# The first three weight slabs of a stage: rounded half of x first, products with the remainder a chunk behind

## The reference

```python
x = layer_norm(DN_ALPHA * x + 0.5 * swiglu(x, ffn1_w_gate[i], ffn1_w_up[i], ffn1_w_down[i]), ...)
y = swa_mixer(x, ...) if kind == 0 else nsa_mixer(x, ...)      # layer 0: sliding window, layer 1: NSA
x = layer_norm(DN_ALPHA * x + y, ...)
x = layer_norm(DN_ALPHA * x + mem_cross_attention(x, mem, ...), ...)
x = layer_norm(DN_ALPHA * x + 0.5 * swiglu(x, ffn2_w_gate[i], ffn2_w_up[i], ffn2_w_down[i]), ...)
```

## Time and profile before

| | |
|---|---|
| median of 3 runs | 2507.37 us (2506.06 to 2510.13) |
| profiled execution | 2509.4 us, span 2507.6 us |
| mean granted clock of PE | 0.964 of full speed |
| PE busy | 2312.6 us, 92% of the span |
| POOL, ACT, DVE busy | 1171.1, 871.6, 839.0 us |
| matmuls | 11164 |

### The profile page before, as it was taken

How to read it: one execution, slowest core, us unless ns; L and a number is a source line. 1 busy time by engine, 2 the same in 40 slices (tenths; PEclk the granted TensorE clock), 3 DMA queues, 4 the chain that set the end, 5 groups by cost and what they waited for, 6 DMA issues and landing times.

```text
span 2507.6 us, 28615 instructions
## 1 busy us (share of the span) xinstructions
PE 2312.6 (92%) x11164; PEld 1942.9 (77%) x11164; DVE 839.0 (33%) x1610; ACT 871.6 (35%) x1505; POOL 1171.1 (47%) x703
## 2 busy tenths in 40 slices
PE   7999997789799799999799999789999798999997
PEld 5888886677687688888688888678887686888886
DVE  2111134456436311113311112446676436211115
ACT  3322233553243322223322223256664243322222
POOL 5454444556446454444354444244446445644442
PEclk9999999999899899999899999899999898999998
DMA  4332332112312233333233332220002312333331
GB/s 162 101 93 93 101 93 85 59 35 76 110 51 84 82 94 101 93 100 93 68 97 97 93 101 89 62 68 18 18 18 69 99 51 76 95 98 97 97 96 56
DMA packets 57734, 204.96 MB, mean 82 GB/s; under 512 B 6912, under 2 KB 7040, under 8 KB 57088
## 3 DMA queue, kind: packets, MB, share of 16 engines
q1 hardware_dynamic: 55728, 196.63, 26.1%
q10 hardware_dynamic: 1872, 6.50, 0.7%
HBM read 201.01 MB, written 2.10 MB: 81 GB/s over the span
## 4 chain that ended last, share of the span: by engine, by line
PE 81%; DVE 8%; POOL 6%; issue 3%; ACT 3%; ACTq 0%; DMA 0%; DVEq 0%; POOLq 0%
PE bank L1211 23%; PE bank L1213 23%; PE bank L1212 23%; POOL w_lo L377 4%; PE bank L1407 2%; DVE t L918 1%; DVE f L894 1%; PE bank L1433 1%; DVE f L886 1%; ACT w_hi L522 1%; PE bank L1434 1%; PE bank L1435 1%; PE bank L1237 1%; PE bank L1239 1%; PE bank L1238 1%
## 5 line engine op out<-in xcount | busy, mean ns | idle before, releaser
L377 POOL TENSOR_TENSOR w_lo<-w_raw,w_hi 128x1024 fp32r<-128x1024 f32 (+1 forms) x379 | 905.0, 2392 | 1055.2 <-ACT w_hi L522 1055.0
L1211 PE MATMUL bank<-x_hi,w_hi 128*128 128x512 f32 x1712 | 681.0, 398 | 78.0 <-DVE memk L937 31.8
L1212 PE MATMUL bank<-x_lo,w_hi 128*128 128x512 f32 x1712 | 676.1, 395 | 0.0
L1213 PE MATMUL bank<-x_hi,w_lo 128*128 128x512 f32 x1712 | 675.7, 395 | 0.0
L522 ACT ACTIVATE w_hi<-w_raw 128x1024 fp32r<-128x1024 f32 (+1 forms) x379 | 390.8, 1036 | 520.5 <-PE bank L1213 504.3
L1211 PEld LDWEIGHTS bank<-x_hi,w_hi 128*128 128x128 f32 x1712 | 327.7, 191 | 149.6 <-POOL w_lo L377 33.6
L1211 PE MATMUL bank<-h_hi,w_hi 128*128 128x512 f32 x960 | 378.7, 395 | 3.7 <-DVE h_lo L1153 2.8
L1213 PEld LDWEIGHTS bank<-x_hi,w_lo 128*128 128x128 f32 x1712 | 327.0, 191 | 69.5
L1212 PEld LDWEIGHTS bank<-x_lo,w_hi 128*128 128x128 f32 x1712 | 327.8, 191 | 64.4
L1212 PE MATMUL bank<-h_lo,w_hi 128*128 128x512 f32 x960 | 374.2, 390 | 0.0
L1213 PE MATMUL bank<-h_hi,w_lo 128*128 128x512 f32 x960 | 374.1, 390 | 0.0
(11 more groups left out here) (197 smaller groups left out, 2620.9 us busy)
## 6 DMA issues: line engine op xcount, KB each, us to landing
w_raw<-w_dram SPq DMA_DIRECT2D x315, 512.0 KB, 3.6
w_raw<-w_dram SPq DMA_DIRECT2D x64, 448.0 KB, 3.3
f<-mem_dram ACTq DMA_DIRECT2D x3, 1024.0 KB, 4.9
t<-x_dram ACTq DMA_DIRECT2D x4, 512.0 KB, 8.4
out_dram<-t SPq DMA_DIRECT2D x8, 256.0 KB, 2.0
f<-cmp_w_dram ACTq DMA_DIRECT2D x1, 1024.0 KB, 6.6
cw<-cmp_w_dram ACTq DMA_DIRECT2D x1, 96.0 KB, 8.7
lng<-ln_g_dram ACTq DMA_DIRECT2D x1, 32.0 KB, 9.3
```

The costliest lines, as they stand in the source:

```text
L377: pool.tensor_tensor(w_lo[:, slot(s), 0:n * P], w_raw[:, s % RAW, 0:n * P], w_hi[:, slot(s), 0:n * P].bitcast(F32), ALU.subtract).then_inc ...
L1211: pe.matmul(dst, w_hi[:, slot(s), w], m_hi[:, k, :], start=k == 0, stop=False)
L1212: pe.matmul(dst, w_hi[:, slot(s), w], m_lo[:, k, :], start=False, stop=False)
L1213: last = pe.matmul(dst, w_lo[:, slot(s), w], m_hi[:, k, :], start=False, stop=k == n - 1)
```

## The change

`together` no longer calls `chunk`. For each chunk k it waits on `xhi_ready` and issues for the three slabs the two products with `x_hi` of chunk k; then it waits on `x_ready` of chunk k - 1 and issues for the three slabs the one product with `x_lo` of chunk k - 1. The loop has a ninth pass, with only the three remainder products of the last chunk; these close the accumulation and raise `slab_done`. The wait on `lo_ready` of a slab stays ahead of its first product. There are 72 products as before, on the same operands; the order in which they are added up in PSUM differs. `together` is called once in each stage.

```diff
--- before.py
+++ after.py
@@ -1220,10 +1220,23 @@
 
             def together(st, group):
 
-                for k in range(KC):
-                    pe.wait_ge(x_ready, KC * st.ln + k + 1)
-                    for s, dst in group:
-                        chunk(s, dst, x_hi, x_lo, k, KC)
+                n0 = KC * st.ln
+                for k in range(KC + 1):
+                    if k < KC:
+                        pe.wait_ge(xhi_ready, n0 + k + 1)
+                        for s, dst in group:
+                            w = slice(k * P, (k + 1) * P)
+                            if k == 0:
+                                pe.wait_ge(lo_ready, s + 1)
+                            pe.matmul(dst, w_hi[:, slot(s), w], x_hi[:, k, :], start=k == 0, stop=False)
+                            pe.matmul(dst, w_lo[:, slot(s), w], x_hi[:, k, :], start=False, stop=False)
+                    if k:
+                        pe.wait_ge(x_ready, n0 + k)
+                        for s, dst in group:
+                            w = slice((k - 1) * P, k * P)
+                            last = pe.matmul(dst, w_hi[:, slot(s), w], x_lo[:, k - 1, :], start=False, stop=k == KC)
+                            if k == KC:
+                                last.then_inc(slab_done, 1)
 
             def token_major(ss, b, i, src_hi, src_lo, width):
```

## The result

The changed kernel takes 2522.22 us (median of 5 runs, 2519.73 to 2524.98), the one before beside it 2508.56 us. The ratio is 1.0055 (95% interval 1.004 to 1.007): slower by 13.7 us, between 10 and 17.6. The profiled execution of after has a span of 2520.2 us, 12.6 more than before, and a mean granted clock of 0.960 in place of 0.964. The forecast was 2514.6 with a range up to 2520: the direction was right, the size is outside the range.

What follows compares the result with a forecast made beforehand. PE, 92% busy, was taken to bound the kernel, starting on x only in stage 7. Terms -1.16 + 3.2 + 2.7 = +4.7 us plus 2.5 for the clock gave 2514.6 us from 2507.4; range 2508.5 to 2520.

Steps and rivals of the forecast that it cites:

- Pace, 0.227 us: In the stage blocks, one product takes 0.227 us at the full clock, across chunk borders and semaphore waits too.
- free semaphore waits: The eight semaphore waits each stage gains cost nothing, because TensorE's queue of issued work hides them.
- (1): Stage 7's start: PE begins on the rounded half of x instead of its remainder, 1.16 us sooner.
- (2): Stop before slab three in seven stages: four products precede it, not six, so 0.45 us each, +3.2 us.
- (3): Slab one released later at the block's end: 0.91 us more in each of stages 1, 2 and 6, +2.7 us.
- slack of 1.8 us in the feed-forward stages: Stages 0, 3, 4, 7: slab four's work covers the late release with 1.8 us to spare, so no cost.
- cover by kw in stage 5: Stage 5: slab kw's product just covers the late release of slab one; 0.1 us at most.
- The rival in which the late slab is swallowed: Stages 1, 2 and 6 have slack behind the late start: only +2.0 us, 2509.4 us; chance 0.15.
- (4): Clock falls behind longer idles: a fall in stage 1 (1.7), half for stages 2 and 6 (0.85), +2.5 us.
- The upper bound, 6.8: Clock cost at most 6.8 us: four falls, both ends of stage 1 and one each in stages 2 and 6.
- the clock falls everywhere: Rival: +4.7 + 6.8 us, with later short idles of the mixers falling too, 2519 us; chance 0.1.
- moved work: The first three terms, at stage 7's start, slab three's stops and slab one's release: +4.7 us without the clock.

Runs made afterwards that it cites:

- e6: Kernel before with, in stages 0 to 6, slabs one and two by chunk and slab three whole behind them; stage 7 in the new order: 2465.93 us, ratio 0.9837.
- e3: Kernel before with only the six middle chunks lagged, first and last chunk whole as before the change: 2508.15 us, ratio 1.0002.
- e2: Changed kernel's start and lag, but the last chunk done whole, slab by slab, so slab one is released as before: 2511.77 us, ratio 1.0017.
- e4: Kernel before with the new order in stage 7 alone: 2504.44 us, ratio 0.9987.
- e5: Changed kernel plus two unread products ahead of slab three's wait, so six stand there again: 2518.7 us, ratio 1.0046.
- g3: Changed kernel plus unread products: two ahead of slab three's wait, 8 behind stage 1's block, 6 behind those of stages 2 and 6: 2514.68 us, ratio 1.0023.
- g1: Kernel before plus four unread products behind the 72 of stage 0, a pure shift of 0.91 us: 2510.67 us, ratio 1.0009.
- g2: Kernel before plus eight unread products behind the 72 of stage 0, a pure shift of 1.8 us: 2505.85 us, ratio 0.9995.
- f2: Kernel before with chunk 0 whole and the rest lagged (late release of slab one) in stages 1, 2 and 6 alone: 2520.24 us, ratio 1.0051.
- f3: As f2, plus unread products behind the block, 8 in stage 1 and 6 in stages 2 and 6: 2516.19 us, ratio 1.0031.
- f1: Kernel before with the late release of slab one in all stages but 1, 2 and 6: 2507.95 us, ratio 1.0002.
- e1: Kernel before with chunk 0 whole and the rest lagged in all stages, so slab one is released late: 2519.25 us, ratio 1.0037.

## Why the prediction was right or wrong

**What bounds the kernel: right.** The change names x, and x was not what PE waits for at seven of eight starts. The waits for weight remainders decided, as `e6` shows from the other side.

**Pace, 0.227 us, and the free semaphore waits: right.** `e3` has the lagged middle and is the kernel before within 0.1%. In after, 51 products behind the stop of stage 4 take 0.227 us each. The 1 us that the range's upper end holds for the semaphore waits is a term that no run shows; `e3` has 48 of the 64 additional waits and bounds them at 2.8 us.

**(1) Stage 7: right.** The first product came 1.94 us behind the start of the rounding of its `x_hi` before (2125.59 against 2123.65) and comes 0.77 us behind it after (2138.32), 1.17 sooner where 1.16 was predicted:

```profile
2137.55 0.72 ACT L619 ACTIVATE x_hi<-t,lnb 128x512 fp32r<-128x512 f32 x1 [3.91 <-DVE t L918]
```

It is 0.77 or 0.78 us in the traces of `e2`, `e4`, `e5` and `g3` as well.

**(2) 0.45 us at each of seven stops: right where it can be seen alone, hidden by the clock elsewhere.** In stage 2 of `g3` and `e5` it is there to the hundredth together with (3). In stages 3, 4 and 5 of after it isn't: the shift is the same behind them as ahead of them. The stop of stage 4 is 0.85 us longer (7.86 against 7.01), because four products end sooner than six, and it ends at the same moment. But the clock came back sooner behind it. (In stage 6 the end of the stop wasn't set by ScalarE and GpSimd alone, as the prediction had it, but in before by the raw slab's DMA too.) In stage 3, first the product at the stop and the 30th behind it in before, then the same two in after:

```profile
831.24 0.79 PE L1211 MATMUL bank<-x_hi,w_hi 128*128 128x512 f32 x1 [3.17 <-POOL w_lo L377]
...
840.98 0.39 PE L1211 MATMUL bank<-x_hi,w_hi 128*128 128x512 f32 x1
```

```profile
842.99 0.80 PE L1231 MATMUL bank<-x_hi,w_hi 128*128 128x512 f32 x1 [4.02 <-POOL w_lo L377]
...
852.25 0.39 PE L1232 MATMUL bank<-x_hi,w_lo 128*128 128x512 f32 x1
```

The same 30 products take 9.74 us before and 9.26 after, 0.48 less, which is what the two additional ones cost. The prediction's clause that they come at the full clock "since the low phase behind a stop passes first" held the low phase to be the same in both orders. Kernels with before's order in stage 3 have it too: these 30 products take 9.47 to 9.49 us in `e4`, `g1` and `g2`, 9.26 in `f2` and 9.23 in `f3`. So the gain needs no change of the order; a term of 0.45 us is smaller than what the clock does behind such a stop from one execution to the next.

**(3) The late release: right as work.** 0.91 us in each of stages 1, 2 and 6 shows in the idles (3.17, 2.39, 2.40, against 2.27, 1.49 and 1.49), and `f1` shows no cost elsewhere, so the slack of 1.8 us in the feed-forward stages and the cover by kw in stage 5 held. The rival in which the late slab is swallowed falls.

**(4) The clock: the step that failed.** It stood in the sum at 2.5 us, the rest in the table is 7.9 of the profiled execution, and 9.0 of the median's 13.7. The prediction's sentence was "I take the first as a fall (1.7) and half a fall for the two together (0.85)". That much was nearly right: 3.17 us of idle in stage 1 gave a fall in each of the four profiled executions that have it, of 1.5 us in after, `e1` and `f2` and of 2.5 in `e5`; 2.27 gave none in seven, and 1.39 none in two. 2.39 to 2.40 gave one of 1.5 in stage 6 in four of four, none in stage 2 in four of four. So 3.0 us against 2.5. What failed is that the clock was priced only at idles that the change makes longer. All other stretches were taken at the clock they had in before, and that isn't theirs to keep: at a stage start with idles of about a microsecond the clock fell in one execution and not in another of the same code (before, `g1` and `e4` in stage 1). After fell at two such places (2.65 and 2.9), lost 1.4 in the mixer of stage 1 and 3.4 in the norm of stage 5, and won at others (1.4, 1.1 and 2.6, of which 1.0 is the DMA in stage 6). Two of these stand in more than one trace: the start of stage 2 in both kernels with four products ahead of the stop (2.9 in after, 1.3 in `e2`), and the norm of stage 5 in seven. The upper bound, 6.8, counted falls at three stages' ends and a start and so had no room for these. The rival "the clock falls everywhere", 2519, was the nearest, at a chance of 0.1, and was short too. That the direction came out right isn't luck: the moved work alone has it, and the clock added to it.

**What stays open.** Each stretch was read in one profiled execution. The falls at the ends of stages 1 and 6 repeat in four kernels; those at the start of stage 2 come with four products ahead of the stop (after, `e2`) and in none of the ten other variants of the same blocks with six, but `e5` in turn lost part of it elsewhere. From the norm of stage 5 (1950.32) to stage 6's slab one it takes 39.6 to 39.7 us in seven of the fourteen traces and 42.9 to 43.1 in the other seven (after, `e1`, `f2`, `f3`, `e5`, `e2` and `g3`), with nothing between and without a cause that was tested. How much of the +2.65 and the +1.4 in stage 1 is the change's is open, as said at the table. Why the idle of 2.4 us falls in stage 6 and not in stage 2 isn't settled.

## What to carry to other kernels

When PE is 92% busy, list every gap of a few microseconds and the granted clock behind it before costing a reorder: the moved work here was 4.7 us, as forecast, and the clock took twice that again. Compare two profiled executions of the same code before you explain a difference of 2 or 3 us between two kernels: here such a stretch differed by 2.5 us with nothing changed. Give a shift of everything behind a change a range of its own, measured by adding a few useless matmuls to the kernel before (here +2.3 and -1.3 us for 0.9 and 1.8 us of work). And when the engine stops for the third of three operands, don't reorder within the three: finish the two that are ready and take the late one behind them, which gave most of the 41 us here.

## What the runs showed of the hardware

- A fall of TensorE's clock to 1.2 GHz cost 1.5 us behind a single idle of 3.17 us (0.72 on the mean of 6 us) and 2.3 to 2.9 us behind two or three idles close together (0.50 to 0.64 of 6 us, the stops of stages 1 and 2).
- At such a place the same code fell in one execution and not in another: with the stop at 421.94 in both, 1.00 in before (1.36 us of idle) and 0.57 in `g1` (1.11 us).
- Whether a slab's DMA had landed moved the end of a stop by 1.0 us, and in all traces with this wait (before, `e3`, `g1`, `e5`) the clock fell behind the stop of stage 6, in none without it.
- Unread matmuls in idles of 2.4 to 3.2 us made the kernel faster, by 4 to 5 us for 20 of them at three places (`f2` to `f3`).
- Idles of no more than 1.3 us each, a few microseconds apart, also brought falls: 0.57 behind the 1.11 us of `g1`, 0.64 behind the 1.29 us of `e4`. The Trainium skill (TensorE: Matmul & The Clock Gate, "A second HAM failure mode: psum-queue depth-cycling") says of a kernel that cycles through PSUM banks that very short idles between its groups of matmuls are frequent enough to make the clock go up and down. The traces agree that idles this short can bring a fall, and add that like ones can be harmless: 1.00 behind 1.35 us in `g2`.
